# Two or three pairs of accumulator banks through the feed-forward phases, and the start of the first up phase, in a two-block transformer kernel

## The reference

```
hn = rmsnorm(x);  x = x + softmax(q k^T) v @ w_o
u = causal_dwconv(rmsnorm(x) @ w_up);  gate, up = split(u)
x = x + (silu(gate) * up) @ w_down;   x = rmsnorm(x)          # end of block one
mod = silu(c) @ w_mod + b_mod                                  # nine vectors of 1024
h = modulate(rms_norm(x), sh1, sc1); x = x + 0.5 (1 + ga1) swiglu(h)
h = modulate(rms_norm(x), sh2, sc2); x = x + (1 + ga2) mixer(h)
h = modulate(rms_norm(x), sh3, sc3); x = x + 0.5 (1 + ga3) swiglu(h)
```

## Time and profile before

| | |
|---|---|
| median of 3 executions | 829.29 us (828.58 to 829.97) |
| profiled execution, its own time | 828.27 us |
| its span | 826.0 us |
| around the span | 2.27 us |
| PE busy | 801.6 us, 97% |
| DVE busy | 644.4 us, 78% |
| ACT busy | 488.3 us, 59% |
| DMA | 179.44 MB, 217 GB/s in the mean |

### The profile page before, as it was taken

One profiled execution on the slowest core, in us unless ns is written; L12 is line 12 of the kernel. 1 busy time (PEld: TensorE's weight loads), 2 busy tenths in 40 slices (PEclk: granted clock), 3 DMA queues, 4 the chain that ended last, 5 costly groups with the idle time before them and its releaser, 6 DMA issues. The chain is left out here.

```text
span 826.0 us, 16828 instructions
## 1 busy us (share of the span) xinstructions
PE 801.6 (97%) x6818; PEld 779.5 (94%) x6818; DVE 644.4 (78%) x1331; ACT 488.3 (59%) x1015; POOL 21.0 (3%) x53
## 2 busy tenths in 40 slices
PE   6999997999999999999999999899999999999998
PEld 5899997999999999999999999879889999999998
DVE  5788877988999886999888887777657897765651
ACT  6755556766666665755554646565655775555440
POOL 1000000000000000000000000700000000000000
PEclk9999999999999999999999999999999999999999
DMA  8776673766565987599998886625333677665540
GB/s 288 257 234 234 198 246 116 248 204 203 192 218 180 321 293 251 154 315 333 344 314 301 288 265 210 190 71 186 113 130 103 205 240 253 222 204 192 191 154 27
DMA packets 150013, 179.44 MB, mean 217 GB/s; under 512 B 5680, under 2 KB 139568, under 8 KB 149936
## 3 DMA queue, kind: packets, MB, share of 16 engines
q1 hardware_dynamic: 148624, 178.17, 65.7%
q0 software_dynamic: 1024, 0.03, 0.1%
q10 hardware_dynamic: 288, 0.16, 0.1%
HBM read 177.27 MB, written 1.05 MB: 216 GB/s over the span
## 5 line engine op out<-in xcount | busy, mean ns | idle before, releaser
L933 DVE TENSOR_TENSOR wlo<-raw,whi 128x512 fp32r<-128x512 f32 x528 | 343.3, 685 | 71.9 <-ACT whi L690 71.1
L1307 PE MATMUL bank<-A,whi 128*128 128x256 f32 x1280 | 364.1, 284 | 14.4 <-DVE wlo L933 7.5
L690 ACT ACTIVATE whi<-raw 128x512 fp32r<-128x512 f32 x528 | 308.3, 622 | 99.5 <-PE bank L1309 95.8
L1308 PE MATMUL bank<-A,whi 128*128 128x256 f32 x1280 | 356.9, 279 | 0.0
L1309 PE MATMUL bank<-A,wlo 128*128 128x256 f32 x1280 | 356.6, 279 | 0.0
L1307 PEld LDWEIGHTS bank<-A,whi 128*128 128x128 f32 x1280 | 243.1, 190 | 17.9 <-DVE wlo L933 9.0
L1308 PEld LDWEIGHTS bank<-A,whi 128*128 128x128 f32 x1280 | 243.2, 190 | 1.0 <-issue 1.0
L1309 PEld LDWEIGHTS bank<-A,wlo 128*128 128x128 f32 x1280 | 243.1, 190 | 0.0
L1307 PE MATMUL bank<-Hhi,whi 128*128 128x256 f32 x528 | 146.0, 276 | 0.0
L1309 PE MATMUL bank<-Hhi,wlo 128*128 128x256 f32 x528 | 145.7, 276 | 0.0
L1308 PE MATMUL bank<-Hlo,whi 128*128 128x256 f32 x528 | 145.7, 276 | 0.0
(11 more groups left out here) (148 smaller groups left out, 783.0 us busy)
## 6 DMA issues: line engine op xcount, KB each, us to landing
mring<-in_w_mod SPq DMA_DIRECT2D x72, 512.0 KB, 6.5
raw<-in_ffn_w_up SPq DMA_DIRECT2D x22, 1024.0 KB, 5.1
raw<-in_w_gate SPq DMA_DIRECT2D x22, 1024.0 KB, 5.7
raw<-in_w_up SPq DMA_DIRECT2D x22, 1024.0 KB, 5.8
raw<-in_w_down SPq DMA_DIRECT2D x16, 1024.0 KB, 5.8
raw<-in_w_in SPq DMA_DIRECT2D x12, 1024.0 KB, 5.7
raw<-in_moba_w_qkv SPq DMA_DIRECT2D x11, 1024.0 KB, 5.5
raw<-in_ffn_w_down SPq DMA_DIRECT2D x8, 1024.0 KB, 6.2
```

The costliest lines, as they stand in the source:

```text
L690: act.activation(whi[:, i % SPL, k0:k1, 0:width], raw[:, i % RAW, k0:k1, 0:width], ACT.Copy).then_inc(s_whi, 1)
L933: dve.tensor_tensor(lo, raw[:, i % RAW, k0:k1, 0:width], hi.bitcast(F32), ALU.subtract).then_inc(s_wlo, 1)
L1307: pe.matmul(o, hi, xh, start=kg == 0 and not (j and halved(g)), stop=False)
L1308: pe.matmul(o, hi, xl, start=False, stop=False)
```

## The change

1. Table load: `norm("up1")` no longer calls `silu()`; the table is loaded where the first Silu of `up1` needs it, behind that group's eviction.
2. First slab of `up1` (`early`): the product of high by high waits for `s_ahi` alone, and `s_alo` is waited for ahead of the second product.
3. `warm`: nine products of the constant `meanf` (128 x 128) into bank 6 between the sums and the first product of `up1`.
4. Banks: groups of the six up and down phases take three pairs in turn, (0, 1), (2, 3) and (5, 6), and the first product of any group waits for the last users of its own banks (`users_before`), which is group g - 3 inside these phases.
5. `MOD_STEPS`: the condition's product at slab 29 of `up1` goes, and slab 50, the last of `down1`, gets one. The steps between move up by one number.

```diff
+THREE, UP_PAIRS = ("up1", "down1", "up2", "down2", "up4", "down4"), ((0, 1), (2, 3), (5, 6))
...
-    "qkv1": lambda i: int(i > 2) + int(i in (4, 7, 10)), "o1": lambda i: int(i < 15), "up1": lambda i: int(i in (29, 33)),
-    "down1": lambda i: int(i < 50), "up2": lambda i: int(i >= 55) * (1 + int(i % 4 == 3)), "down2": lambda i: int(i < 83),
+    "qkv1": lambda i: int(i > 2) + int(i in (4, 7, 10)), "o1": lambda i: int(i < 15), "up1": lambda i: int(i == 33),
+    "down1": lambda i: int(i < 51), "up2": lambda i: int(i >= 55) * (1 + int(i % 4 == 3)), "down2": lambda i: int(i < 83),
...
                 if norm == "up1":
                     st.put("norm", norm)
+                    st.put("warm")
...
+            if groups[g][0] in THREE:
+                return banks[pair_of(g)[i]][:, c0:c1]
...
+        def pair_of(g):
+            begun, turn = ("up4", 0) if groups[g][0] in ("up4", "down4") else ("up1", 2)
+            return UP_PAIRS[(g - plan.group_of[plan.first_of[begun]] + turn) % 3]
+
+        def banks_of(g):
+            if groups[g][1] == "o" and groups[g][2] >= 2 * C:
+                return (O_BANKS[groups[g][2]],)
+            if groups[g][0] in THREE:
+                return pair_of(g)
+            return (2 * (g % 2),) if halved(g) else (2 * (g % 2), 2 * (g % 2) + 1)
+
+        def users_before(g):
+            return [max((h for h in range(g) if b in banks_of(h)), default=-1) for b in banks_of(g)]
...
-                if ph in ("up1", "up2", "up4"):
+                if ph in ("up2", "up4"):
                     silu()
...
+                if high:
+                    need.wait_ge(s_ahi, 8 * NORM_OF[ph] + kg + 1)
+                    return Ahi[:, kg, :], Alo[:, kg, :], S
...
-                xh, xl, ncol = here(tag, ph, kg, g)
+                early = i == plan.first_of["up1"]
+                xh, xl, ncol = here(tag, ph, kg, g, early)
...
-                    emptied(need, g - 2)
+                    for before in users_before(g):
+                        emptied(need, before)
...
                     pe.matmul(o, hi, xh, start=kg == 0 and not (j and halved(g)), stop=False)
+                    if early:
+                        here(tag, ph, kg, g)
                     pe.matmul(o, hi, xl, start=False, stop=False)
...
+            def warm():
+                for _ in range(9):
+                    pe.matmul(banks[T_BANK][:, 0:P], meanf[:, :], meanf[:, :], start=True, stop=True)
```

4 lines of the change are left out of this document (2 added, 2 removed).

## The result

The changed kernel takes 823.78 us (median of 5 runs, 822.80 to 825.79), the kernel before 828.58 us beside it (5 runs, 827.71 to 829.97). The ratio is 0.9941, with a 95% interval of 0.9926 to 0.9956: 4.8 us less, 3.6 to 6.1 by the interval. The prediction was 825.4 us, its range 824.2 to 827.7.

The account below looks back on a forecast made before the run. PE, busy 97% of the span, was taken as the bound. The start of `up1` (0.97 us) and the banks (2.91) sum to 3.88 us; taken from the median 829.29 this gives 825.4 us, range 824.2 to 827.7.

Parts of the forecast that it names:

- The start of `up1`: Slabs 16 to 18: without the table load DVE's chain moves 0.77 us forward and slab 18 starts 0.97 us earlier.
- the 0.2 us that the prediction gave to the clock: Slab 17: the clock's fall before the change was nearly free, 0.2 us of it showed (0.97 against 0.77).
- The banks: Slabs 34, 55, 56 and 107: waiting for g - 3 removes the bank waits and the excess behind them, 2.91 us.
- The table load at its new place: Behind the first Silu's eviction: DVE stands about 1.4 us, slab 19's low part has 3 us of cover, cost nothing.
- The product of the condition: One product of 1.22 us moves from `up1` to the end of `down1`: nothing gained, up to 0.1 us lost.
- the last of the sum: Final step: subtract the gain from the median 829.29, the profiled execution being 1.02 us faster than it, giving 825.4 us.
- the clock falls at another place: Rival: the new 1.4 us wait at k tile 6 may lower the clock in later slabs; gain 2.3 us, chance 0.13.
- The wait for the banks does not come back: Denies a rival: bank waits return whole through another wait on the late DVE; gain 0.97 us, 828.3 us, chance 0.07.
- DVE takes nothing back: Denies a rival: spacing stays wide or busy DVE before 380 us takes some back; gain 2.4 to 3.1 us, chance 0.20.
- PE is bound by itself: Rival at slab 18: it starts where PE is ready, about 139.1; gain 5.3 us in all, 824.0 us, chance 0.06.
- The slower rival: Rival: third pair or slab 17's split waits put long stretches in wider spacing, 0.2 us per slab; chance 0.04.

Follow-up runs that it names:

- the kernel that changes the order: The changed kernel with the last low part of slab 17 put ahead of the eight `Alo` tiles: 823.78 us, ratio 0.9926.
- the resets: The kernel before with more one-column products, at slabs 110 and 111 of `up4`: 830.35 us, ratio 0.9999.
- `up4` only: The kernel before with three pairs of banks in `up4` and `down4` alone: 829.17 us, ratio 0.9987.
- the kernel that kept the wait: The changed kernel with its three pairs of banks, but each group also waits for g - 2 as before: 828.36 us, ratio 0.9991.
- `up1` to `down2`: The kernel before with three pairs of banks in the four phases `up1` to `down2`, two in `up4` and `down4`: 826.29 us, ratio 0.9957.
- the products at slab 89: The changed kernel with nine more constant products in PE's pause ahead of slab 89 in `qkv3`: 823.05 us, ratio 0.9908.

## Why the prediction was right, and where it was short

**The start of `up1`: right.** 0.97 us forecast, 0.87 measured (the lead of 1.02 less the 0.15 from ahead of slab 16), with the wait where it should be, 1.05 us of it shown and 1.33 from start to start for 1.4. Its parts 2 and 3 are under the cover of that wait, as costed: without the high parts first the two slabs take 18.86 us, without the constant products 18.89, with both 18.86. Only the table load counts: moved alone it gives 0.75 us at this place; the 0.2 us that the prediction gave to the clock measured 0.12. That the wait comes from the order of the list is shown by the kernel that changes the order: slab 17 at 6.41 us.

**The banks: right in one execution.** 2.91 us forecast, 2.77 between the two traces and 2.77 with three pairs alone; slabs 34 and 56 at the 5.58 us that was forecast, slabs 55 and 107 at 5.54 for 5.44, since their first products stand behind one-column products, which I had not counted.

**The table load at its new place: the cost of nothing is right, the cover named for it was the wrong one.** I checked only the low part of slab 19, with 3 us. With the wait for g - 2 the load costs 0.64 us at slab 20, by a late eviction; it is free because of the third pair. Two edits that I costed apart hang together.

**The product of the condition:** nothing was seen of it; it was not tried alone.

**The step that failed** is the last of the sum: "That execution is 1.02 us faster than the median of 829.29, so the median of the changed kernel should be 829.29 - 3.9". The profiled execution of the changed kernel came out at the 824.39 us of the sum, but the median lies 0.61 us below it and not 1.02 above: 1.63 us, which is the whole distance from 825.4 to 823.78. Seen as base and gain, 0.7 of it is the base (829.29 was the median of three executions, that of the five beside the changed kernel is 828.58) and 0.9 the gain (4.8 for 3.9). The time that the profiled execution of before lacked against its median is not a constant that both kernels carry. It has two parts, one in each kernel.

In the kernel before, part of it is the wide state behind a wait for the banks, of which the sum held only the 0.77 us of slabs 55 and 56, read from one execution that had no long stretch of it. Nine traces of this study are of kernels that still wait for g - 2 in some of these phases. In seven of them there are wide stretches beyond slabs 55 and 56: the table load alone (slabs 31 to 33 and 108 to 116, 2.6 us), the constant products alone (1.9), the resets (3.2), `up4` only (0.8), the kernel that kept the wait (0.5), and before again (1.7) and again (1.0). In two, before's first and `up1` to `down2`, there are none. Over the nine that is a mean of 11.7 / 9 = 1.3 us; over the six that wait in every phase, as before does, 10.4 / 6 = 1.7. In the seven traces with three pairs in all six phases and slab 17's wait left in place (the changed kernel three times, and without constant products, without high parts first, with the pairs alone, with the products at slab 89) there is none. So the term of the banks is 2.8 us and some 1.3 to 1.7 on the mean, where it was put at 2.91.

In the changed kernel the profiled execution had the fall in slab 89, which costs 1.6 us and which by the granted clocks at least two of its five executions did not have. That is the other half of "the clock falls at another place". The fall of before in slab 17, "nearly free: 0.2 us of it showed", cost 0.12 us by one pair of traces, and 0.77 more in a trace in which it lasted longer. The changed kernel has no fall in slab 17 in any of its three traces.

**What the clock's part is** can be bounded, since the granted clock of every execution is on record. Of 104 executions of the kernel before on the five chips, 21 are at 0.997 or 0.998, 47 at 0.996 and 36 at 0.995 or less. The last group is 0.9 us slower than the middle one, each execution taken against the mean of its chip; spread over all, 0.3 us. At one and the same clock the rest of the gain is still there. At 0.998 the kernel before has a median of 828.76 us (19 executions) and the kernel with three pairs alone 824.07 (3 executions): 4.7 us, where the slabs give 2.8. At 1.000 the kernel with the constant products alone takes 826.38 to 830.46 us (9 executions, median 827.01, mean 827.81), the changed kernel 822.80 to 823.50 (6 executions, median 823.11, mean 823.13): 3.9 us by the medians and 4.7 by the means, where the slabs of the two traces without a long stretch give 3.5. Falls of the clock can't make a spread of 4.1 us at 1.000, and it is gone with the wait for g - 2. These groups are small and mix chips.

Sum by these: 0.87 + 2.77 + 1.3 to 1.7, and 0.3 for the clock, is 5.2 to 5.6 us. The three comparisons gave 4.8, 6.8 and 6.8 us, and one kernel against itself was off by 1.6 us once. That fits. What is not shown is that the wide stretches make up the whole of the rest: it rests on nine traces and the groups above. Nor do the traces show the fall in slab 89 to be rarer with three pairs: 4 of 8 have it, leaving out those with products ahead of it, and 5 of 9 of the others.

On the later chips the median of before was 828.9 to 830.9. A range of 824.2 at its low end left only 1.2 us below the forecast, all that rows of one execution gave; the fall in slab 89 alone moves an execution by 1.6.

**The rivals.** The wait for the banks does not come back in three-pair kernels. DVE takes nothing back. The new wait ahead of k tile 6 did not lower the clock: in the eight traces that have it (0.93 to 1.06 us idle) it is 1.00 from 133 us up to slab 89. But the rival's remark that one wait may lower the clock in one execution and not in another came true at slab 89, which the forecast had not looked at. That PE is bound by itself was wrong for the list as it stands and right for the other order: the low part put first gave 1.2 us more at slab 17. The slower rival (the wide state in long stretches) has the right mechanism and the wrong sign: it was in the kernel before, and the change took it away. Only where slab 17 was sped up does it appear with three pairs, and it takes 1.05 of the 1.2 us.

**Open:** what puts PE in the wide state and what ends it. Read by the spacing inside each slab, the traces hold nineteen wide stretches beyond the first slabs of the phases. Fifteen of them end at a slab that begins with one-column products, three end at slab 56, which has none, and one at the norm ahead of slab 51. Four times the state ran on past such products (slab 39 once, 57 once, 109 twice), so they mostly end it, and not always. It began behind a wait for a bank in most traces, behind a hitch of 0.04 us in slab 30 of the table load alone, and without an idle row where the low part came first. At slab 55 it is the state of slabs 51 to 54 that goes on: in all eight traces with two pairs there the one-column products stand behind a wait and slab 55 is wide, in the twelve with three pairs there is no wait and the state ends. Whether the constant products help the kernel before isn't settled either; they do raise its granted clock.

## What to carry to other kernels

A short wait of PE costs more than its idle row: price the slabs behind it over several executions, not one, and a change that takes short waits away can give back more than the trace shows it to lose. When a load or a long instruction is moved, follow not only its own consumer but whatever is queued behind that consumer on the waiting engine; here the eviction, not the weights, was without cover. Before trusting a few tenths of a per cent, run the kernel against itself. And a profiled execution is one draw: what separates it from the median must be found in each kernel, not carried from one to the other.

## What the runs showed of the hardware

- Products of 256 columns run in one of two steady spacings, 113.3 ns (5.44 us for 48) and 117.7 ns (5.65 us), for many slabs at a time; the granted clock is 1.00 in both, and no row shows an idle time. The same program enters the wide one at different places in different executions, and leaves it at one-column products in 15 cases of 19.
- The clock after a pause of PE: with 3.24 or 3.25 us of idle time ahead of slab 17 it was lower in that slab in all seven traces, and with 2.48 us (the table load alone) as well, seven times at 0.72 to 0.74 over 6 us (133 to 139), once at 0.51 over 7 us. With 2.03 us of idle time it was 1.00 in the one trace, but no execution of that kernel has a mean above 0.998. In slab 89, behind a wait of 2.06 us in the first trace, the same kernel had it at 0.81 over 9 us in one execution and at 1.00 in another; over all kernels it fell there in 9 traces of 20. Without the nine constant products ahead of slab 17 one execution of 158 reached a mean granted clock of 0.999, with them 45 of 72.
- The table load took 1.28 us, and the next ACTIVATE started 0.01 us behind its end (143.68 + 1.28 = 144.96, and 144.97).
- The constant products are f32, two rows each: their 18 rows of 128 columns start 0.112 us apart (2.17 us in all), the f32 rows of 256 columns ahead of them 0.216, and the rows of 256 columns with fp32r operands 0.113.
